# One double modulation unit moves from the first down projection to the second, in exchange for a single one

## The reference, cut to what matters

```python
def conv_glu_ffn(h, w_up, conv_w, conv_b, w_down):
    S = h.shape[1]
    a, b = jnp.split(h @ w_up, 2, axis=-1)
    a_pad = jnp.pad(a, ((0, 0), (CONV_WIDTH - 1, 0), (0, 0)))
    a = sum(conv_w[j] * a_pad[:, j:j + S] for j in range(CONV_WIDTH)) + conv_b
    return (jax.nn.silu(a) * b) @ w_down
```

```python
def adaln(cvec, w_mod, b_mod):
    return jnp.split(jax.nn.silu(cvec) @ w_mod + b_mod, 6, axis=-1)

sh1, sc1, gt1, sh2, sc2, gt2 = [m[:, None] for m in adaln(c, w_mod[l], b_mod[l])]
csh1, csc1, cgt1, csh2, csc2, cgt2 = adaln(c_ctx, w_mod[l], b_mod[l])
```

## Time and profile before

| | |
|---|---|
| median of 3 runs | 2236.97 us (2235.26 to 2238.47) |
| the profiled execution | 2236.31 us, span 2234.5 us |
| TensorE busy | 2037.2 us, 91% of the span |
| VectorE busy | 1132.5 us, 51% |
| POOL busy | 864.7 us, 39% |
| ScalarE busy | 678.0 us, 30% |
| reductions of the modulation (L1076) | 64, 115.6 us, 1806 ns in the mean |
| mean granted TensorE clock | 0.957 of full speed |

### The profile page before, as it was taken

The page is one execution under the profiler, slowest core; times in us unless marked ns, Lnnn a source line. Parts: engine busy times, 40 slices in busy tenths (PEclk is TensorE's granted clock), DMA queues, the critical chain, the costliest instruction groups (busy, mean ns, idle before and its releaser), DMA issues.

```text
span 2234.5 us, 26112 instructions
## 1 busy us (share of the span) xinstructions
PE 2037.2 (91%) x9716; PEld 1619.9 (72%) x9716; DVE 1132.5 (51%) x2106; ACT 678.0 (30%) x1071; POOL 864.7 (39%) x648
## 2 busy tenths in 40 slices
PE   4989789999999979999999999779998978999997
PEld 3766467787788766567888888568876757888886
DVE  7778873535733867655335333373333446312334
ACT  4242562321122235543211221224444222212211
POOL 4343004445644731124446445132221423444442
PEclk9999999999999989999999999699999989999998
DMA  4222002423522520013226223121120212223321
GB/s 161 80 86 86 13 13 79 150 96 114 214 94 89 203 94 13 24 48 132 106 76 218 103 84 109 60 76 57 57 76 1 94 57 76 88 78 116 104 71 71
DMA packets 32064, 199.16 MB, mean 89 GB/s; under 512 B 3681, under 2 KB 3809, under 8 KB 14049
## 3 DMA queue, kind: packets, MB, share of 16 engines
q1 hardware_dynamic: 27072, 166.74, 21.3%
q10 hardware_dynamic: 4896, 31.15, 3.9%
HBM read 195.78 MB, written 2.10 MB: 89 GB/s over the span
## 4 chain that ended last, share of the span: by engine, by line
PE 50%; DVE 5%; ACT 1%; issue 1%; POOL 1%; DVEq 0%; ACTq 0%
PE psum L1409 43%; PE psum L1431 2%; PE psum L1595 1%; PE psum L1532 1%; PE psum L1560 1%; PE psum L1577 1%; DVE work L970 1%; PE psum L1831 1%; DVE work L974 1%; POOL w_lo L557 1%; DVE h_lo L953 1%; DVE xT L965 0%; DVE work L959 0%; DVE work L948 0%; PE psum L1523 0%
## 5 line engine op out<-in xcount | busy, mean ns | idle before, releaser
L557 POOL TENSOR_TENSOR w_lo<-raw,w_hi 128x512 fp32r<-128x512 f32 (+2 forms) x640 | 856.2, 1367 | 1340.9 <-ACT w_hi L587 1340.9
L1409 PE MATMUL psum<-h_hi,w_hi 128*128 128x512 f32 x1560 | 615.6, 395 | 11.7 <-DVE a_q L1002 4.5
L1409 PE MATMUL psum<-h_hi,w_lo 128*128 128x512 f32 x1560 | 612.5, 393 | 0.0
L1409 PE MATMUL psum<-h_lo,w_hi 128*128 128x512 f32 x1560 | 612.1, 392 | 0.0
L587 ACT ACTIVATE w_hi<-raw 128x2048 fp32r<-128x2048 f32 (+2 forms) x176 | 301.5, 1713 | 584.5 <-PE psum L1409 488.8
L1409 PEld LDWEIGHTS psum<-h_hi,w_hi 128*128 128x128 f32 x1560 | 294.8, 189 | 85.1 <-issue 14.8
L1409 PEld LDWEIGHTS psum<-h_hi,w_lo 128*128 128x128 f32 x1560 | 294.5, 189 | 63.8 <-issue 2.4
L1409 PEld LDWEIGHTS psum<-h_lo,w_hi 128*128 128x128 f32 x1560 | 294.7, 189 | 62.6 <-issue 2.3
L1409 PE MATMUL psum<-g_hi,w_hi 128*128 128x512 f32 x528 | 207.0, 392 | 8.5 <-issue 5.0
L1409 PE MATMUL psum<-g_lo,w_hi 128*128 128x512 f32 x528 | 205.6, 389 | 0.0
L1409 PE MATMUL psum<-g_hi,w_lo 128*128 128x512 f32 x528 | 205.5, 389 | 0.0
(11 more groups left out here) (273 smaller groups left out, 2488.7 us busy)
## 6 DMA issues: line engine op xcount, KB each, us to landing
raw<-w_up SPq DMA_DIRECT2D x66, 1024.0 KB, 4.8
raw<-w_dn SPq DMA_DIRECT2D x48, 704.0 KB, 4.1
mod_w<-w_mod ACTq DMA_DIRECT2D x24, 1024.0 KB, 4.9
raw<-w_c_in SPq DMA_DIRECT2D x13, 1024.0 KB, 4.8
raw<-w_b_in SPq DMA_DIRECT2D x7, 1024.0 KB, 4.8
raw<-w_a_idx SPq DMA_DIRECT2D x5, 1024.0 KB, 5.5
raw<-w_a_out SPq DMA_DIRECT2D x8, 640.0 KB, 3.9
raw<-w_b_out SPq DMA_DIRECT2D x8, 640.0 KB, 3.8
```

The lines of the kernel that those rows point to most:

```text
L557: ins = nc.gpsimd.tensor_tensor(LO[slot][:, a:z], RAW[slot][:, a:z], HI[slot][:, a:z].bitcast(F32), ALU.subtract)
L1409: ins = nc.tensor.matmul(out, l, r, start=(k == 0 and m == 0), stop=(k == n - 1 and m == 2))
```

## The change

The order in which the 24 modulation units are taken becomes a list. Units 7 and 8 change places: the last place beside `dn00` (n = 7) now has unit 8, a single one, and the first place beside `dn01` (n = 8) has unit 7, a double one. Loads, buffers and semaphores go by the place n, the weights, the number of reductions and the column of the result by the unit u. Line numbers behind the edit are 2 or 3 higher in the changed kernel.

```diff
--- before.py
+++ after.py
@@ -338,6 +338,8 @@
             split += n
         order = [PH[s[0]] for s in STREAM]
         MOD_PHASES = ["dn00", "dn01", "dn10"]
+
+        MOD_ORDER = [*range(7), 8, 7, *range(9, 24)]
 
         raw_landed = [sem("raw_landed0"), sem("raw_landed1")]
         hi_ready, lo_ready = sem("w_hi_ready"), sem("w_lo_ready")
@@ -808,7 +810,7 @@
             stream_only(PH["a_out"])
 
             def load_mod(u):
-                act.dma_start(MODW[u % 2][:], wdram["mod"][u].rearrange("p (c n) -> p c n", c=2)).then_inc(
+                act.dma_start(MODW[u % 2][:], wdram["mod"][MOD_ORDER[u]].rearrange("p (c n) -> p c n", c=2)).then_inc(
                     mod_landed[u % 2], 16)
 
             def ffn(l, first):
@@ -1066,18 +1068,19 @@
                     if steps[s]["last"]:
                         flush(s)
 
-            def mod_unit(u):
-
-                if u == 0:
+            def mod_unit(n):
+
+                u = MOD_ORDER[n]
+                if n == 0:
                     v.wait_ge(cond_ready, 1)
-                v.wait_ge(mod_landed[u % 2], 16 * (u // 2 + 1))
+                v.wait_ge(mod_landed[n % 2], 16 * (n // 2 + 1))
                 for c in range(2):
                     for w in range(2 if u < 8 else 1):
-                        ins = nc.vector.tensor_tensor_reduce(TW[:, 4 * S:4 * S + D], MODW[u % 2][:, c, :], COND[:, w, :],
+                        ins = nc.vector.tensor_tensor_reduce(TW[:, 4 * S:4 * S + D], MODW[n % 2][:, c, :], COND[:, w, :],
                                                              1.0, 0.0, ALU.mult, ALU.add, MODV[:, 2 * u + c, w:w + 1])
                         if c == 1 and (w == 1 or u >= 8):
                             ins.then_inc(mod_used, 1)
-                            v.wait_ge(mod_used, u + 1)
+                            v.wait_ge(mod_used, n + 1)
                         else:
                             step(ins)
```

## The result

The changed kernel takes 2240.56 us (median of 12 runs, 2239.1 to 2241.3) against 2235.91 us for the kernel before in the same comparison (12 runs, 2234.07 to 2238.47). The ratio is 1.0019, 95% interval 1.001 to 1.0028: slower by 4.65 us where 2.05 us was forecast. The profiled execution took 2240.38 us with a span of 2238.6 us, 4.1 us over that of before.

What follows compares the result with a forecast made beforehand. TensorE, busy 2037.2 of 2234.5 us, was taken as the bound, so VectorE edits matter only where it waits. Removal 0 and addition 2.05 us on the median of 2236.97 gave 2239.0 us, range 2236.2 to 2241.8.

Steps and rivals of the forecast that it cites:

- The removal costs and gains nothing: End of dn00: two reductions fewer at n = 7 leave the 3.56 us wait before up01 as it was; gain 0.
- the cover I named: TensorE's first unit of up01 hides the second unit's weights, 0.84 us early before, 3.4 us early after.
- The double unit ends at 735.50: VectorE at the start of dn01: n = 8, with four reductions, ends at 735.50 instead of 732.29, 3.2 us later.
- the rule of the Trainium skill weighed in the prediction: VectorE and POOL: shared ports are an exclusive lock held to an instruction's end; a proportional split would give about 2.3 us.
- Unit 3 of dn01 starts 2.05 us late: TensorE in dn01 waits 2.1 us for w_lo and starts unit 3 at 743.03 instead of 740.98.
- The far bound of 3.0 us: dn01: if w_lo of unit 3 met reductions all the way, it would end at 743.9, a delay of 3.0 us.
- The clock stays up: TensorE behind dn01's new 2.1 us wait: matmuls not slowed, as after earlier waits of 1.68 and 2.75 us.
- the first rival: The clock falls at dn01's new wait, costing 1.5 us more, 2240.5 us in all; chance 20%.
- Nothing is given back: Rest of dn01 and behind: units 5 and 7 also start 2.05 us late, and nothing recovers the delay.
- The delay does not repeat: dn01: no second wait at unit 4 or 5; the rival, a repeated delay giving 2241.1 us, had 9%.

Runs made afterwards that it cites:

- 2: Kernel before with the unit at n = 8 also given four reductions, n = 7 left double: 2240.64 us against 2236.73, ratio 1.002.
- experiment 7: Kernel before with double unit 7 moved to the last place, n = 23, behind dn10; dn01 all single: 2236.74 us against 2236.60, ratio 1.0004.
- 9: Kernel before with only a small memset added at VectorE's start: 2233.26 us against 2236.63, ratio 0.9988.
- 11: Kernel before with 12 unread filler matmuls ahead of TensorE's 3.56 us wait before up01: 2232.78 us against 2236.63, ratio 0.9986.
- 1: Kernel before with two of four reductions removed at n = 7, a memset at VectorE's start, nothing added in dn01: 2233.38 us against 2236.73, ratio 0.9989.
- 12: Changed kernel with w_hi ahead of the reload in dn01 and 12 filler matmuls before up01: 2233.40 us against 2236.63 for the kernel before, ratio 0.9985.
- 5: Changed kernel with TensorE's dn01 code written out in place of a loop: 2240.25 us against 2236.60 for the kernel before, ratio 1.0019.
- 6: Changed kernel, TensorE's dn01 written out, 9 unread matmuls ahead of its wait for unit 3: 2238.59 us against 2236.60 for the kernel before, ratio 1.0008.
- 4: Kernel before with ScalarE making w_hi ahead of the reload in dn00, dn01 and dn10: 2237.63 us against 2236.73, ratio 1.0003.
- 3: Changed kernel with ScalarE making w_hi ahead of the modulation reload in dn01 only: 2235.24 us against 2236.73 for the kernel before, ratio 0.9989.

## Why the prediction was right or wrong

The side was right, and the place and the mechanism of the delay too; that the clock would stay up was not. The size was 2.05 us where the medians give 4.65 us and the spans 4.1 us. Step by step:

*The removal costs and gains nothing.* Held for this kernel: the wait before up01 stayed at 3.56 us, dn01 began after 190.44 us as before, the addition alone (2) is as slow as the whole change, and experiment 7 is the same as before. But the cover I named, TensorE's first unit of up01, was 0.84 us long only because the clock had fallen in it. In experiments 9 and 11, with the clock up, TensorE waited 1.64 and 0.70 us for the second unit; with a single unit at n = 7 (1, 12) it did not, and up to dn01 the removal was worth 2.01 us (1 against 9). A slack measured inside a slow stretch is worth only as much as that stretch.

*The double unit ends at 735.50.* Held within 0.02 us. Both the order with POOL's last piece and the lengths of all four reductions came out, and w_lo of unit 2 was not stretched (5.68 us), as it would have been if the two engines shared a port in proportion. That agrees with the rule of the Trainium skill weighed in the prediction ("SBUF — State Buffer", "Who interferes with whom").

*Unit 3 of dn01 starts 2.05 us late.* Mis-sized: 25.59 us after dn01's first matmul against 22.83, 2.76 us. Two terms of the sum were too small. I carried over 0.44 us from reload to w_hi; it took 0.72 us (736.83 - 736.11), and 0.72 to 0.73 us in experiments 2, 5 and 6 as well, for a reason not shown. And I had w_lo end 5.33 us after the addition of VectorE. POOL began at 738.29, and the reduction at 738.28, 0.01 us ahead of it, ran in 1.23 us with POOL behind it; so w_lo took 5.98 us where the sum has 5.57 (737.40 to 742.97), and ended at 744.27. The start 0.30 us later (738.29 - 0.59 = 737.70 on the clock of before, forecast 737.40) and the 0.41 us make up the 0.71 us that 2.76 has over 2.05. The far bound of 3.0 us held.

*The clock stays up.* Failed; this was the first rival, at 20%. The new wait was 2.69 us by the trace and the clock fell, while one of 2.75 us and those of 2.81 and 2.78 us in experiments 1 and 9 left it up. In experiment 5 one of 2.78 us made it fall again, as long to the hundredth as that of experiment 9. Its price was 1.63 us (6), forecast 1.5. I had ordered waits by length and read a threshold into three rows. They hold none; what decides between waits of this length is not shown. That the rival's time, 2240.5 us, is the one measured is in part luck: its base, a median of 3 runs, was 1.06 us above that of 12 (2236.97 and 2235.91), and its change was 3.55 us against 4.65.

*Nothing is given back.* Held in dn01, not behind it. 2.76 + 1.63 = 4.39 us. The first thing to give some back is TensorE's wait for VectorE's sum of squares, shorter by 0.39 us behind the late unit, before and after:

```profile
781.69 1.05 PE L1518 MATMUL psum<-ones,work 128*128 128x1 f32 x8 [1.36 <-DVE work L1086]
```

```profile
786.26 1.05 PE L1521 MATMUL psum<-ones,work 128*128 128x1 f32 x8 [0.97 <-DVE work L1089]
```

These two stand 253.98 and 257.96 us after dn00's first matmul, 3.98 us apart, and so does the start of the projection after dn01 (793.90 - 528.30 = 265.60 against 789.33 - 527.71 = 261.62). By the start of the last down projection (2159.64 and 2155.60) it is 3.45 us. The two spans' 4.1 us is this and the 0.59 us ahead of dn00. The medians' 4.65 us lies above it, within their interval of 2.2 to 6.3 us (0.001 and 0.0028 of 2236).

*The delay does not repeat.* Held: one wait only, and one of 0.16 us before unit 5, which starts 42.55 us after dn01's first matmul (761.29 - 718.74) against 38.24.

## What to carry to other kernels

When an engine waits for a slow helper in order to reload a buffer, and makes something urgent afterwards, the helper's length is on the path; issue the urgent work first, and check what TensorE meets next when it gets there sooner (4 moved its waits, 3 didn't). Price a slack only together with the clock of the stretch that it was read in, and put a wait of a few us on TensorE down at its length plus the fallen clock, as two cases near each other in chance. For an effect of 3 us test a control that adds one idle instruction, and read in the traces where each gains: here the control's median was worth as much as the edit, and its trace was not.

## What the runs showed of the hardware that I had not expected

A reduction on VectorE and a subtraction on POOL went by who came first, to hundredths of a us: started 0.01 us ahead of POOL it took 1.23 us, 0.05 us behind it 2.32 us (1). One such order changed POOL's unit from 8.7 to 7.9 us and the wait from 3.56 to 2.8 us, and behind the shorter wait the clock stayed up (granted 1.00 over 4.3 us in 1 and 9, in place of 0.64 before).

Waits of TensorE of about 2.7 us went either way: behind 2.69 us (the changed kernel, 2) and 2.78 us (5) the clock was low (granted 0.55 over 3.8 us), behind 2.75 us (before), 2.78 us (9) and 2.81 us (1) it was up (1.00).

The two groups of run times in experiment 3 differ in the mean granted clock as well: 0.958 to 0.961 in the six shorter runs, 0.957 to 0.958 in the six longer ones. That points at the clock and not at the timer, though no profile of the second group was taken.
